# Twelve slots for expert weights and a reordered mixer tail in a two-layer hybrid trunk

## The chip, the cores and the metric

The kernel runs on one core of a Trainium2 chip. The metric is the device time of one execution in microseconds (us): 994.39 is the median of three runs of the kernel before (994.18 to 998.19). All arithmetic is float32.

## The reference

Two groups of 128 tokens, a prompt (g = 0) and latent tokens (g = 1), go through DEPTH = 2 layers of width 1024. Both groups use the same weights, so the kernel carries them side by side. One layer is:

```python
mod = silu(cond) @ w_ada[l] + b_ada[l]           # 6 parts of 1024: sh1, sc1, g1, sh2, sc2, g2
hn  = rmsnorm(x, norm_mix[l]) * (1 + sc1) + sh1
proj = hn @ w_in[l]                              # 3840 columns, split for three mixers
# differential attention (8 heads), retention (4), HGRN2 (4); each ends in an rmsnorm,
# retention and HGRN2 also times silu of a gate (r_g, g_g)
mix = concat(o_da, o_ret, o_hg) @ w_out[l]
x   = x + g1 * mix
hn  = rmsnorm(x, norm_ffn[l]) * (1 + sc2) + sh2
# router shared by all layers: 16 experts in 4 groups; the group with the largest sum of its two
# best scores, then its two best experts
x   = x + g2 * sum_e gate[e] * (silu(hn @ w_gate[l, e]) * (hn @ w_up[l, e])) @ w_down[l, e]
```

## The kernel before

**Weights.** All large weights go through `ring`, RING = 8 slots of 128 partitions x 2048 floats (1.049 MB each). SyncE issues every load (`load`, L353) in one fixed order, into slot `n % 8`, after the slot's last use has been counted; TensorE takes slots in the same order (`slot`, L430). The order in a layer is: w_in's blocks f, q, a, b, i, r, v, s with w_ada steps between them (ADA_BEHIND), the rest of the w_ada steps (LATER), w_out in eight half-filled slots, w_ada steps for the next layer (IN_ROUTER), and 96 expert slots. At the change of layers AT_CHANGE = 6 further w_ada steps come first (`at_change`, L551). A w_ada step (`ada_step`, L508) is one load and four products with a moving side of 512 columns.

**Engines.** Each engine runs its own list in the order in which it is written; semaphores tie the lists together, and after nearly each step an engine waits for its own result. PSUM has eight banks; projections and transposes of the mixers take banks 2, 3 and 0 in turn (`next_bank`, L574), scores take 4 to 7. There is no planner: the orders are written out by hand, TensorE's from L788 on, VectorE's from L1344, ScalarE's from L1706.

**Around the mixers.** The norm is folded into products: ScalarE squares and sums a group's rows (`squares`, L1585), VectorE scales a unit matrix by the result (`normed`, L1055), and TensorE multiplies x by this diagonal, which also transposes it (`normalized`, L478). VectorE and ScalarE shift and scale the result by feature into `hnT` (`shifted`, L1072 and L1607). Both groups are done one after the other before block f begins.

**The mixers' tail** (TensorE L864 to L885, VectorE L1391 to L1425, ScalarE L1742 to L1755). When the last values are there, `gated_norm` and `da_norm` fill `xs` with the mixed rows; `transposed("mix", ...)` (L873) turns them, in banks 0 and 3; VectorE copies group 0 and ScalarE group 1 to `hnT`; `copied("mix")` waits for all; then four sweeps of 256 columns for each group multiply by w_out, and VectorE adds `g1 * mix` to x, one quarter at a time. In layer 1 the second modulation (`modulation_by_feature`, L875) stands between the two groups' transposes.

**The turns.** The router gives each token two experts and a seat among 64 in each. The loop from L935 on does eight turns of two experts. A turn gathers the tokens of both experts (`gather`, a product with a 0/1 matrix), multiplies by w_gate and w_up (the two experts on the two halves of TensorE's columns), transposes the activations, multiplies by w_down, gathers for the next turn, and scatters the turn before it (`scatter`) into banks 4 to 7 in between. Each turn uses 12 slots: four of w_gate, four of w_up, four of w_down. The activation (VectorE L1515 to L1521) lies between w_up and w_down.

**After the turns** VectorE computes `x += g2 * y` in four pieces of 512 columns, two steps each (L1532 to L1540). Then the next layer's norm begins, or ScalarE issues the two output stores (L1783).

## Time and profile before

| what | before |
|---|---|
| median of 3 runs | 994.39 us |
| profiled execution, whole | 995.69 us |
| its span, first to last instruction | 993.9 us |
| granted TensorE clock, mean | 0.979 |
| PE busy | 932.2 us (94%) |
| PEld (weight loads into the array) busy | 507.4 us (51%) |
| DVE busy | 433.8 us (44%) |
| ACT busy | 158.8 us (16%) |
| POOL busy | 58.8 us (6%) |
| DMA | 303.63 MB, mean 305 GB/s |

The busy shares are averages over stages that are bound by different things. In the page's 40 slices of about 25 us, DMA moves 421 GB/s in the two long stretches in which the turns run and far less in the mixers of layer 1, while VectorE's share is high in the mixers and low in the turns. A busy matmul row can hide a short wait, since ends of matmuls are modelled; the chain of waits names such time "issue". In all rows times are in us from the start of the span, unless marked ns. PE is TensorE's matmuls, DVE VectorE, ACT ScalarE, POOL GpSimd, SPq SyncE's queue. A row's line (L421) can be that of a helper: L421 is every product, L454 every transpose, L361 every load of the ring. A float32 product is two instructions.

### The profile page before, as it was taken

How to read it: one execution, taken by the hardware profiler on the slowest of the kernel's cores; microseconds unless marked ns; L12 is line 12 of the kernel's file. 1: busy time of each engine (PE TensorE's matmuls, PEld its weight loads, DVE VectorE, ACT ScalarE, POOL GpSimd, SP SyncE). 2: the span in 40 equal slices, each digit the busy share in tenths (PEclk: the TensorE clock that was granted, in tenths of full speed). 3: DMA queues.
4: the chain of work that ended last, by engine and by line, in shares of the span. 5: the costliest groups of instructions: out<-in, count | busy, mean ns of one | idle time of the engine just before them, and what ended most of it. 6: DMA issues, size and time to landing. Idle time of an engine off the chain costs nothing.

```text
span 993.9 us, 13356 instructions
## 1 busy us (share of the span) xinstructions
PE 932.2 (94%) x5182; PEld 507.4 (51%) x5189; DVE 433.8 (44%) x792; ACT 158.8 (16%) x408; POOL 58.8 (6%) x92
## 2 busy tenths in 40 slices
PE   6899999999899999999989998998979999999996
PEld 2655574577543444443447567557863444443442
DVE  1386878533322222122347987863252222122222
ACT  2211043211100001010020203331120001010000
POOL 1112220020000000000000322000000000000000
PEclk9899999999999999999999999997989999999999
DMA  9997566478799999999996323312627999999992
GB/s 371 368 401 265 212 223 246 154 261 315 316 377 421 421 421 421 421 421 421 421 420 253 107 92 122 112 50 83 254 85 298 421 421 421 421 421 421 421 420 98
DMA packets 49582, 303.63 MB, mean 305 GB/s; under 512 B 7808, under 2 KB 7824, under 8 KB 17136
## 3 DMA queue, kind: packets, MB, share of 16 engines
q1 hardware_dynamic: 43520, 291.52, 72.7%
q0 software_dynamic: 2960, 8.63, 2.5%
q10 hardware_dynamic: 3040, 2.62, 0.8%
q8 instruction: 42, 0.69, 0.3%
q14 instruction: 20, 0.16, 0.0%
HBM read 300.10 MB, written 2.65 MB: 305 GB/s over the span
## 4 chain that ended last, share of the span: by engine, by line
PE 74%; DVE 16%; DMA 3%; ACT 3%; issue 3%; another core or an unknown queue 0%; SPq 0%; DVEq 0%; ACTq 0%
PE ps L421 72%; DMA ring<-in_w_ada 3%; PE ps L454 2%; ACT eP L1557 2%; DVE A L1235 1%; DVE rt L1033 1%; DVE xy L1229 1%; DVE eP L1333 1%; DVE stat L1033 1%; DVE eP L1331 1%; DVE F L1154 1%; DVE sq L1188 1%; DVE hnT L1081 0%; DVE proj L1262 0%; DVE xy L1160 0%
## 5 line engine op out<-in xcount | busy, mean ns | idle before, releaser
L421 PE MATMUL ps<-ring,proj 128*64 128x512 f32 x1536 | 339.4, 595 | 9.8 <-issue 8.0
L421 PEld LDWEIGHTS ps<-ring,proj 128*64 128x64 f32 x1536 | 109.8, 137 | 215.9 <-issue 213.9
L421 PE MATMUL ps<-ring,hnT 128*128 128x512 f32 (+1 forms) x576 | 204.5, 508 | 2.1 <-ACT hnT L1755 1.9
L421 PEld LDWEIGHTS ps<-ring,hnT 128*128 128x128 f32 x576 | 108.3, 193 | 75.8 <-issue 65.7
L421 PE MATMUL ps<-hnT,ring 128*64 128x128 f32 (+2 forms) x576 | 73.3, 338 | 0.0
L421 PEld LDWEIGHTS ps<-proj,xs 128*128 128x128 f32 x512 | 62.6, 203 | 16.0 <-issue 16.0
L421 PE MATMUL ps<-proj,xs 128*128 128x128 f32 x512 | 65.6, 290 | 4.2 <-issue 2.4
L421 PEld LDWEIGHTS ps<-hnT,ring 128*64 128x64 f32 (+1 forms) x576 | 59.9, 158 | 11.8 <-issue 2.4
L421 PE MATMUL ps<-proj 128*128 128x512 f32 x128 | 61.5, 606 | 0.0
L421 PE MATMUL ps<-ring,silT 128*32 128x512 f32 x384 | 48.3, 618 | 12.3 <-DVE silT L1049 7.5
L1527 DVE COPY proj<-ps 128x512 f32<-128x512 f32 x16 | 11.1, 692 | 109.1 <-PE ps L421 109.1
L1516 DVE TENSOR_SCALAR proj<-proj 128x512 f32<-128x512 f32 x16 | 6.8, 427 | 112.5 <-ACT proj L1557 112.5
L1517 DVE RECIPROCAL proj<-proj 128x512 f32<-128x512 f32 x16 | 53.6, 3353 | 0.5
L1569 ACT COPY proj<-ps 128x512 f32<-128x512 f32 x24 | 14.1, 586 | 161.7 <-PE ps L421 161.7
L421 PEld LDWEIGHTS ps<-proj 128*128 128x128 f32 x128 | 21.9, 190 | 29.2 <-issue 29.2
L421 PEld LDWEIGHTS ps<-xy 64*128 64x128 f32 (+1 forms) x480 | 30.0, 188 | 12.7 <-issue 11.8
L421 PE MATMUL ps<-xy 64*128 64x64 f32 (+1 forms) x480 | 32.2, 275 | 0.7 <-issue 0.6
L1777 ACT COPY proj<-ps 128x512 f32<-128x512 f32 x16 | 9.4, 586 | 146.3 <-PE ps L454 146.3
L1774 ACT COPY proj<-ps 128x512 f32<-128x512 f32 x32 | 18.8, 586 | 73.0 <-PE ps L421 73.0
L1235 DVE COPY_PREDICATED A<-c_later,ps 128x256 f32<-128x256 int32 x56 | 29.2, 521 | 1.9
L1557 ACT ACTIVATE eP<-ps,rt 128x128 f32<-128x128 f32 (+1 forms) x64 | 26.2, 418 | 23.6 <-DVE rt L1317 22.9
L1524 DVE COPY proj<-ps 128x256 f32<-128x256 f32 x16 | 6.8, 424 | 51.2 <-PE ps L454 51.2
(222 smaller groups left out, 751.2 us busy)
## 6 DMA issues: line engine op xcount, KB each, us to landing
ring<-in_w_gate SPq DMA_DIRECT2D x64, 1024.0 KB, 13.6
ring<-in_w_up SPq DMA_DIRECT2D x64, 1024.0 KB, 12.2
ring<-in_w_down SPq DMA_DIRECT2D x64, 1024.0 KB, 11.4
ring<-in_w_ada SPq DMA_DIRECT2D x48, 1024.0 KB, 8.3
ring<-in_w_in SPq DMA_DIRECT2D x28, 1024.0 KB, 7.5
ring<-in_w_out SPq DMA_DIRECT2D x16, 512.0 KB, 4.4
ring<-in_w_in SPq DMA_DIRECT2D x4, 512.0 KB, 12.6
xy<-gates POOLq DMA_DIRECT2D x4, 512.0 KB, 5.1
```

What stands on the lines that cost most here:

```text
L421: ins = nc.tensor.matmul(*a, **k)
L454: last = nc.tensor.transpose(ps[:, b, i * P:(i + 1) * P], src, C["ident"][:])
L1033: return v.tensor_reduce(out=out, in_=in_, axis=AX, op=op)
L1154: st(v.reciprocal(R, R))
L1188: st(v.reciprocal(e, e))
L1229: st(tt(keep, keep, other.broadcast_to([P, HR, P // (2 * b), b]), ALU.mult), "hX", g, lv + 1)
L1235: v.copy_predicated(out=half_blocks(A[:, g], lv, 1 - r), mask=mask, data=ps[:, bank, 0:256].rearrange("p (h n b) -> p h n b", h=HR, b=b)). ...
L1517: st(v.reciprocal(ge, ge))
L1527: v.tensor_copy(ys[:, 1], ps[:, 3]).then_inc(c.freed(("yP", 1), "ys", 1), 1)
L1557: return act_(out, in_, AF.Exp, scale=scale, **k)
L1569: (nc.scalar.copy(out, src) if fn is None else fn(src)).then_inc(c.freed(read, *label), 1)
L1774: evac(("xT", half), None, "xTs", half, fn=lambda src: nc.scalar.copy(xT[:, KH * half:KH * (half + 1), :], src.rearrange("p (k s) -> p k s ...
```

## The change

- **Slots.** The turns use twelve slots in the fixed order 4 to 11, 0 to 3: the eight of the ring and four made of buffers that are free during the turns (half of `eP`, `wT`, `F` with `A`, and `xy`, which holds the first gate until the first residual). SyncE waits for the first residual of group 1 before it issues the turns' loads. w_out is laid out as two halves of 512 columns, in four full slots; a slot is swept for two quarters.
- **w_ada.** AT_CHANGE becomes 5, and three steps instead of two stand behind block r in layer 1. Behind block v the steps go ahead of the end state. In the router's stage the steps are split 3, 1, 2, 2 instead of 2, 1, 1, 3, 1.
- **Norms group by group.** `normalized` becomes `normalized_group`. At the change of layers group 1 is normed between the halves of block f's first part. Before the router, VectorE builds group 0's diagonal ahead of the last residual step and group 1's after the first shifted half.
- **Mixers and tail.** VectorE does `query_columns(0)` ahead of `rotated_maps(1)` and evacuates block s ahead of `da_norm(1, 0)`; ScalarE takes the exponential for r_g of group 1 straight from PSUM. Layer 1's second modulation moves to where layer 0 has it. Group 0's transposes go to banks 6 and 7, ahead of the w_ada steps and the end state; each group's columns are copied half by VectorE, half by ScalarE; the first sweep of group 0 goes ahead of the transposes of group 1.
- **Router.** The group score is the largest of the six sums of two scores (three steps) instead of seven steps of minima and maxima.
- **Turns.** Seven products of zeros stand between the last rows and the loop. The gather for turn 1 goes into turn 0, behind w_up; from turn 1 on it stays behind w_down.
- **Second residual.** VectorE does the four products and the two sums of the upper halves, GpSimd the two sums of the lower halves. Each output store waits for its own group.

```diff
+TURN_SLOTS = (4, 5, 6, 7, 8, 9, 10, 11, 0, 1, 2, 3)
-ADA_BEHIND = ((2, 3, 3, 3, 3, 2, 3, 2), (0, 0, 0, 0, 0, 2, 0, 0))
-AT_CHANGE = 6
+ADA_BEHIND = ((2, 3, 3, 3, 3, 2, 3, 2), (0, 0, 0, 0, 0, 3, 0, 0))
+AT_CHANGE = 5
...
+            if s < RING:
+                return ring[:, s].rearrange("p k n -> p (k n)")
+            return (eP[:, 1], wT[:].rearrange("p a n -> p (a n)"), fa[:], xy[:].rearrange("p a h t -> p (a h t)"))[s - RING]
...
-                for i in range(4):
+                for half in range(2):
                     for r in range(2):
-                        load(lambda s: flat_slot(s)[:, 0:KH * 256], ap["w_out"][l, i, r])
+                        load(flat_slot, ap["w_out"][l, half, r])
                 if l + 1 < L:
                     for step in IN_ROUTER:
                         load_ada(*step)
+                sp.wait_ge(c.of("x1", 1), c.at("x1", 1))
...
+            def normalized_group(stage, factors, g, ahead=None, first=None):
+
+                xv = x[:, g].rearrange("p (k q) -> p k q", k=KC)
+                for h in range(2):
+                    b = claim_for_norm() if h or first is None else first
+                    if not h:
+                        if ahead is not None:
+                            ahead(b)
+                        pe.wait_ge(c.of(factors, g), c.at(factors, g))
+                    for k in range(KH):
+                        last = mm(ps[:, b, k * P:(k + 1) * P], xv[:, KH * h + k, :], diag[:, g, :], start=True, stop=True)
...
-                    normalized("hn1", "xn1", (at_change, None))
+                    normalized_group("hn1", "xn1", 0, at_change)
...
                     for g in range(NG):
+                        if l and g:
+                            normalized_group("hn1", "xn1", 1)
                         for hl in range(2):
...
                 da_weights(1, 0)
+                ada_behind("v")
                 end_state(1, "h", T_GI)
-                ada_behind("v")
...
-                if not l:
-                    modulation_by_feature(l, 1, next(turn_of_banks))
+                modulation_by_feature(l, 1, next(turn_of_banks))
...
                 ret_values(1)
+                transposed("mix", "mixed", 0, (6, 7))
                 ada_steps(len(LATER[l]))
                 end_state(0, "r", T_RV)
-                transposed("mix", "mixed", (0,))
-                if l:
-                    modulation_by_feature(l, 1, 2)
-                transposed("mix", "mixed", (1,))
-                copied("mix")
...
                 for n in range(4):
+                    if not n % 2:
+                        ss = [slot(), slot()]
+                    if not n:
+                        copied_group("mix", 0)
+                    out_of(n, 0, ss)
+                    if not n:
+                        transposed("mix", "mixed", 1)
+                        copied_group("mix", 1)
+                    out_of(n, 1, ss)
...
+                stream_zeros(0, 5)
+                mm(ps[:, 0, :], zeros[:, 0:P], zeros[:, 0:BLK], start=True, stop=True).then_inc(c.fills(0, "idle"), 1)
+                mm(ps[:, 0, :], zeros[:, 0:P], zeros[:, 0:BLK], start=True, stop=True).then_inc(S("bank0_free"), 1)
                 pe.wait_ge(S("rounds"), l + 2)
...
                         if t:
                             scatter(t - 1, 0)
-                            led.turn = t
+                        else:
+                            gather(1)
+                        led.turn = t
...
-                        if t + 1 < TURNS:
+                        if t and t + 1 < TURNS:
                             gather(t + 1)
...
+                query_columns(0)
                 rotated_maps(1)
-                query_columns(0)
...
+                evac_block("s")
                 da_norm(1, 0)
-                evac_block("s")
...
                 da_norm(1, 1)
+                mixed_columns(0)
                 gated_norm("ro", rnorm, 1, 24, 512, T_RG, "mixed", 1)
+                mixed_columns(1)
                 for n in range(4):
                     for g in range(NG):
                         sl = slice(n * 256, (n + 1) * 256)
+                        if n == 3 and g:
+                            normed("xn2", 0)
...
-                normed("xn2")
-                shifted("hn2", 1)
+                shifted("hn2", 1, ((0, 0),))
+                normed("xn2", 1)
+                shifted("hn2", 1, ((0, 1), (1, 0)))
...
+                dve.wait_ge(c.of("gate2"), c.at("gate2"))
                 for g in range(NG):
-                    for h in range(2):
+                    for h, to in enumerate((first_product[g], nsq[:])):
                         dve.wait_ge(c.of("y", 2 * g + h), c.at("y", 2 * g + h))
+                        tt(to, ps[:, 4 + 2 * g + h], gbuf2[:, g, h * BLK:(h + 1) * BLK], ALU.mult).then_inc(c.freed(("y", 2 * g + h), "x2p", g, h), 1)
                         dve.wait_ge(S(c.last[0]), c.last_value())
+                    st(tt(x[:, g, BLK:D], x[:, g, BLK:D], nsq[:], ALU.add), "x2", g)
...
+                    gathered(0)
                     for t in range(TURNS):
                         led.turn = t
                         acte.wait_ge(c.of("gu", 0), c.at("gu", 0))
                         st(ex_(ge, ps[:, 2], -1.0), "gexp")
+                        if not t:
+                            gathered(1)
+                            led.turn = t
                         evac(("actT",), None, "actTs", fn=lambda src: nc.scalar.copy(actT, src.rearrange("p (k s) -> p k s", k=KE)))
                         evac(("yP", 0), ys[:, 0], "ys", 0)
+                        if t and t + 1 < TURNS:
+                            gathered(t + 1)
...
+                    for g in range(NG):
+                        pool.wait_ge(c.of("x2p", g, 0), c.at("x2p", g, 0))
+                        put(g_.tensor_tensor(x[:, g, 0:BLK], x[:, g, 0:BLK], first_product[g], ALU.add), "x2a", g)
```

## Rows read from the trace of the kernel before

**Rows 1.** Windows of turns: length, PE, PEld, DVE, ACT, POOL busy, PEclk, DMA, GB/s

```profile
278.00:513.00 235.00, 227.99 (x1115) 96.30 (x1112) 64.41 (x86) 25.15 (x44) 0.00 (x0) 1.00 1.01 421
...
754.00:972.00 218.00, 211.71 (x1034) 91.17 (x1031) 57.47 (x75) 21.79 (x37) 0.00 (x0) 1.00 1.01 421
```

**Rows 2.** Chain that ended last, in order of time: start, length, what.

```profile
287.38 26.65 PE ps L421 x132
...
494.87 3.59 PE ps L421 x15
...
498.85 14.29 DMA ring<-in_w_ada
...
764.07 26.65 PE ps L421 x132
...
793.10 21.24 PE ps L421 x112
...
843.92 0.62 issue
...
972.75 7.07 PE ps L421 x32
```

**Rows 3.** Timeline: w_ada steps at the change; SyncE's first loads in turn 0.

```profile
506.45 3.64 PE L421 MATMUL ps<-ring,silT 128*32 128x512 f32 x32
...
751.20 4.62 SPq L361 DMA_DIRECT2D ring<-in_w_down  x4
```

**Rows 4.** Timeline, layer 1's norm and router; in brackets the idle time before.

```profile
719.61 2.02 PE L421 MATMUL ps<-t,x 128*128 128x128 f32 x16 [1.49 <-DVE t L1058]
...
732.37 0.17 DVE L1440 TENSOR_TENSOR rt<-rt 128x8 f32<-128x8 f32 x1
```

**Rows 5.** Timeline, first gathers, one in the steady state, turn 0's transposes.

```profile
265.49 5.42 PE L421 MATMUL ps<-proj,xs 128*128 128x128 f32 x32 [2.39 <-issue]
...
741.10 6.49 PE L421 MATMUL ps<-proj,xs 128*128 128x128 f32 x32 [1.82 <-DVE proj L1490]
...
762.30 0.88 PE L454 MATMUL ps<-c_begin,proj 128*128 128x128 f32 x6 [0.82 <-DVE proj L1521]
...
829.63 3.84 PE L421 MATMUL ps<-proj,xs 128*128 128x128 f32 x32
```

**Rows 6.** Timeline of TensorE, gaps in the mixers of both layers.

```profile
171.04 1.10 PE L421 MATMUL ps<-proj,kd 128*128 128x64 f32 x8 [1.58 <-DVE proj L1196]
...
606.71 2.09 PE L421 MATMUL ps<-kT,qT 32*128 32x128 f32 x32 [2.65 <-DVE qT L1305]
...
661.12 0.92 PE L454 MATMUL ps<-c_begin,eP 128*128 128x128 f32 x4 [1.93 <-DVE proj L1196]
...
662.27 4.85 PE L421 MATMUL ps<-ring,hnT 128*128 128x512 f32 x8
```

**Rows 7.** Timeline of TensorE, tail of the mixers, layer 0, then layer 1.

```profile
211.54 27.86 PE L421 MATMUL ps<-ring,hnT 128*128 128x256 f32 x128 [0.99 <-ACT hnT L1755]
...
679.10 1.94 PE L454 MATMUL ps<-c_begin,xs 128*128 128x128 f32 x8 [2.34 <-DVE xs L1287]
...
685.62 1.94 PE L454 MATMUL ps<-c_begin,xs 128*128 128x128 f32 x8 [1.38 <-DVE hnT L1415]
...
688.48 29.65 PE L421 MATMUL ps<-ring,hnT 128*128 128x256 f32 x128 [0.91 <-ACT hnT L1755]
```

**Rows 8.** GpSimd's products by form, then timeline: a collision, and the end.

```profile
L1833 POOL TENSOR_TENSOR e<-F 128x512 f32<-128x512 f32 x2 | 2.1, 1038 | 357.8 <-DVE xy L1175 357.8
...
572.98 0.67 POOL L1844 TENSOR_TENSOR xy<-xy,e 128x256 f32<-128x256 f32 x1 [3.96 <-PE ps L421]
...
573.02 0.91 DVE L1229 TENSOR_TENSOR xy<-xy,e 128x256 f32<-128x256 f32 x1 [1.18 <-PE ps L421]
...
988.80 0.69 DVE L1540 TENSOR_TENSOR x<-x,t 128x512 f32<-128x512 f32 x1
...
989.90 0.45 ACTq L1785 DMA_DIRECT2D out_o_ys<-x  x1
```

More of the change, by code:

```diff
@@ L457, in bank_of_transposes, with transposed @@
                 last.then_inc(c.fills(b, *label), 1)
-            def transposed(stage, rows, groups):
-                for g in groups:
-                    pe.wait_ge(c.of(rows, g), c.at(rows, g))
-                    xv = xs[:, g].rearrange("p (k q) -> p k q", k=KC)
-                    for h in range(2):
-                        bank_of_transposes((stage + "T", g, h), [xv[:, 4 * h + k, :] for k in range(4)])
+            def transposed(stage, rows, g, banks=(None, None)):
+                pe.wait_ge(c.of(rows, g), c.at(rows, g))
+                xv = xs[:, g].rearrange("p (k q) -> p k q", k=KC)
+                for h in range(2):
+                    bank_of_transposes((stage + "T", g, h), [xv[:, 4 * h + k, :] for k in range(4)], banks[h])
             def stream_zeros(b, n):
@@ L497, in copied_group @@
                     pe.wait_ge(c.of(stage + "S", g, h), c.at(stage + "S", g, h))
-            def copied(stage):
-                for g in range(NG):
-                    copied_group(stage, g)
             for b in range(8):
@@ L966, in _ @@
                             for half in range(2):
-                                pair = [slot(), slot()]
+                                pair = [slot(TURN_SLOTS[4 * i + 2 * half + e]) for e in range(2)]
                                 pe.wait_ge(c.of("xTs", half), c.at("xTs", half))
@@ L970, in _ @@
                                     for e, s in enumerate(pair):
-                                        last = mm(ps[64 * e:64 * e + 64, 2 + i, :], xT[:, KH * half + k, 64 * e:64 * e + 64], ring[:, s, k, :], start=(half == 0 and k == 0), stop=(half == 1 and k == KH - 1), skip_group_check=True)
+                                        last = mm(ps[64 * e:64 * e + 64, 2 + i, :], xT[:, KH * half + k, 64 * e:64 * e + 64], by_k(s, BLK)[:, k, :], start=(half == 0 and k == 0), stop=(half == 1 and k == KH - 1), skip_group_check=True)
                                         if k == KH - 1 and not (half and e):
@@ L992, in _ @@
                         for half in range(2):
-                            pair = [slot(), slot()]
-                            rows_of = [ring[:, s].rearrange("p k n -> p (k n)").rearrange("p (k n) -> p k n", k=KE // 2) for s in pair]
+                            pair = [slot(TURN_SLOTS[8 + 2 * half + e]) for e in range(2)]
+                            rows_of = [flat_slot(s).rearrange("p (k n) -> p k n", k=KE // 2) for s in pair]
                             for h in range(2):
@@ L1770, in _, with gathered @@
                     step[0] = "act_turn"
-                    for t in range(TURNS):
+                    def gathered(t):
                         led.turn = t
@@ L1902, in laid_out @@
     out = {"w_in": np.concatenate([halves(w_in[:, :, col:col + n], KH).reshape(L, -1) for _, col, n in IN_BLOCKS], 1)}
-    w_out = np.asarray(inputs["w_out"]).reshape(L, D, 4, 256).transpose(0, 2, 1, 3)
-    out["w_out"] = halves(w_out, KH).reshape(L, 4, 2, P, KH * 256)
+    w_out = np.asarray(inputs["w_out"]).reshape(L, D, 2, BLK).transpose(0, 2, 1, 3)
+    out["w_out"] = halves(w_out, KH).reshape(L, 2, 2, P, KH * BLK)
     for n in ("w_gate", "w_up"):
```

202 lines of the change are left out of this document (101 added, 101 removed).

## The prediction

> **What bounds the kernel now.** I read a table by stage first, then the chain of waits, and last the timeline around each idle stretch of TensorE. TensorE is busy in nearly all of the span, so what a change can win is its idle time, its slow-clock time, and whatever it waits for while it still counts as busy. The two stretches of expert turns (about 278 to 513 us and 754 to 972 us) have the DMA engines at a share of 1.01 and 421 GB/s beside a TensorE that is 97% busy [rows 1]. Which of the two sets the pace there? The chain shows it. The down projections of turns 0 and 1 of layer 1 start at 764.07 and 793.10, 29.03 us apart: that is TensorE's own pace. Later, "issue" pieces such as 0.62 us at 843.92 appear in the middle of the up projection, where nothing but a slot that has not landed can hold it. Over all seven periods layer 0 takes 494.87 - 287.38 = 207.5 us and layer 1 takes 972.75 - 764.07 = 208.7 us, against 7 x 29.03 = 203.2 [rows 2]. A turn loads 12 slots of 1.049 MB; at 421 GB/s that is 2.49 us each, 29.9 us a turn. So loads bind the turns by some 0.8 us each, and after layer 0 they still bind: the chain goes 14.29 us through a w_ada load before layer 1's first norm [rows 2].
> Outside the turns DMA has time to spare. There the chain alternates between TensorE and VectorE, and TensorE shows gaps at a handful of places, told below, with its clock at half beside some of them.
>
> **The change part by part.** I place each term on the profiled execution (995.69 us with what lies around its span of 993.9; the median of the runs shown is 994.39, 1.3 lower).
>
> *Twelve slots.* Before, the ring is eight deep: in layer 1 the first four loads after the ring was filled are issued only at 751.20, after the first gate half of turn 0 [rows 3], so DMA stood still before that. After, SP waits for the first residual and then has twelve slots for a turn. Is that wait harmful? In layer 1 it holds back 96 loads to about 22 us before the first gather (719.1 against 741.10, where the x1 sum ends about 0.5 us before the row at 719.61 [rows 4, 5]). 96 x 2.49 = 239 us after x1 the last load has landed. TensorE needs it, at its own pace, about 19 (to the first gather) + 4 (gather) + 26 (turn 0) + 174 (six turns at 29.03) + 22 us = 245 us after x1. Loads are ahead by some 4 us at the narrowest place. In layer 0 two w_ada loads go ahead of them and five behind (103 x 2.49 = 256 us), against about 261 us at which TensorE needs the last w_ada. So the turns should go at 29.03: -4.3 us in layer 0 and -5.5 in layer 1. Bounds: 0 (loads still bind) and these. I take the full value, since the margin comes out positive in both layers.
>
> *The change of layers.* AT_CHANGE of 5 takes one w_ada load out of the bound stretch and puts it behind block r, where its eight matmuls (0.9 us) lie in time that TensorE waits anyway. With loads on time TensorE's own work decides: the w_ada steps can begin 506.45 - 494.87 = 11.6 us after the last down does and take 0.91 each, 16.2 for five, in place of 498.85 + 14.29 - 494.87 = 18.3 and one step of 1.1 after it: -3.2 [rows 2, 3]. Norming group 1 between the halves of block f leaves VectorE's shifts of group 0 bare ahead of the first half; I give 0.9 back for that. Together -2.3 (0 to -4).
>
> *Mixers.* Layer 0: the three w_ada steps moved ahead of the end state cover the 1.58 us wait at 171.04: -1.6 (bounds 0 and -1.6). Layer 1: query_columns(0) ahead of rotated_maps(1) takes away the 2.65 us gap at 606.71, but VectorE (the swish reciprocals and the maxima) is next on that chain and is not shortened; only about 0.5 survives. Evacuating block s before da_norm(1, 0) takes the 1.93 us gap at 661.12, which layer 1's modulation product now fills; what is won is the clock, since the eight instructions after it took 4.85 us, where layer 0's 27.86 / 128 for 256 columns would make it 3.5: I take -1.2 [rows 6, 7]. Together -3.3, bounds 0 and -7.
>
> *Tail of layer 1's mixers.* From the end of the end state (679.10 - 2.34 = 676.8) to the end of the output projection (688.48 + 29.65 = 718.1) it is 41.4 us: waits of 2.34, 1.38 and 0.91, a modulation product of 3.2 (681.04 to 684.24) at half clock, two transposes of 1.94 each, and 29.65 of sweeps [rows 7]. After: group 0's transposes go to banks 6 and 7 and needn't wait for the gated norm of group 1; the modulation product is gone from here; the first sweep covers the norm of group 1. What is left is two transposes at full clock (2 x 1.3), one wait for the copies (0.99, as at 211.54 in layer 0) and sweeps at layer 0's 27.86: 31.5. That is -9.9. Bounds: -4 (only the modulation product leaves) and -11. Layer 0 has no such gaps, its w_ada steps fill them: 0. w_out's four full slots move the same bytes and are long there when needed: 0.
>
> *Norms and router.* With the norm group by group, layer 1's first diagonal is ready when the last sweep ends (the wait of 1.49 us at 719.61 goes), and the second about 0.5 earlier: -1.9. The seven small VectorE steps of the group scores are 0.2 us apart each and three replace them: -0.75. In layer 0 w_ada steps lie in the gaps, so -0.5 for the norms, -0.7 for the scores, and +1.0 for the step that is moved behind the seat count and there delays the last rows: -0.2. Sum -2.8 [rows 4], bounds -1 and -4.
>
> *Entry to the turns.* The first gather takes 5.42 and 6.49 us, while one in the steady state takes 3.84 [rows 5]: half clock after an idle wait. Seven zero products now stand in the wait. They cost 7 x 0.214 = 1.5 us, of which a part lies beside the loop entry (a gap of 1.8 to 2.4 us before those two gathers); I charge 0.9. So -1.6 + 0.9 and -2.65 + 0.9: -2.5. Bounds: +3.0 (the zeros in full, clock no better) and -4.3.
>
> *Turn 0.* The gather of turn 1 moves into the wait for `act` (0.82 before 762.30, and 0.9 between that row's end and 764.07 [rows 2, 5]), and ScalarE's two more copies delay the transposed activations by about half a microsecond: -1.2 for each layer, -2.4. Bounds +1 and -3.4.
>
> *Second residual.* VectorE has six steps of 0.72 us instead of eight. GpSimd's sum of 128x512 is 1.04 us [rows 8] and each can run beside VectorE's next product: -1.45 if nothing collides. The collision is seen in the trace: a 128x512 step of VectorE takes 0.69, so half the size should take about 0.4, but the 128x256 product with both inputs in SBUF took 0.91 at 573.02 as GpSimd's 0.67 us product ran at 572.98. I charge 0.8 for two such. The second group's store is now issued 0.4 us behind the last sum (989.90 against 989.49) and ends the span 4.0 us later, with the prompt's store beside it; with that one sent ahead it goes at once and lands alone, for which I take 1.5, a guess. Together -2.2, bounds -0.5 and -3.
> The Trainium skill, SBUF — State Buffer, Who interferes with whom, says that a VectorE instruction with two SBUF inputs and a GpSimd one that reads SBUF exclude each other, and that the products out of PSUM don't take part. By that rule both of VectorE's sums wait for GpSimd's; without it the end would come 0.8 us sooner. The trace's 0.91 agrees.
>
> Sum: -9.8 - 2.3 - 3.3 - 9.9 - 2.8 - 2.5 - 2.4 - 2.2 = -35.2, so 960.5 for that execution and **959 us** as a median.
>
> **Rivals.**
> *Loads still bind the turns.* For: the margins above are only 4 to 5 us in 240, and SP now issues no turn load before x1. Against: DMA idle time before the turns shrinks on both sides. Then turns and change give nothing: 959 + 12.1 = 971.
> *The mixers' chain catches the gain.* VectorE or ScalarE become late in the tail (both now copy mixed columns between steps of the gated norms). The mixers give 0 and the tail half: 959 + 3.3 + 5 = 967.
> *Only the outer edges move.* The reordering has a new wait in the mixers that eats as much as the tail gives, the loads are no longer early, and only norms, entry and end are left: 984 to 994.
> *Slower: the clock.* TensorE without its pauses is granted half clock in part of the turns. A us spent at half clock does the work of half a us, as gathers of 6.49 and 3.84 show [rows 5]. To eat 35 us it takes 70 us of turns at the lower level; a quarter of both stretches (116 us) would cost 58 us: 1017. Against: in both stretches the clock reads 1.00 at 97% busy [rows 1]. The lower level is seen only behind gaps.
>
> **How the numbers follow.** Forecast (all terms near their value, 950 to 965) 0.62; loads still bind 0.13; the chain catches 0.15; edges only 0.06; slower 0.04. Range 950 to 974: it takes in the first three. A measurement here tells 0.5% (5 us) from no change: faster 0.93, same 0.03, slower 0.04.
>
> **What would show it.** In the trace of after: downs 29.0 us apart in all seven periods of both layers and no "issue" piece of 0.6 us in the up projection; no w_ada load of many us in the chain at the change; no idle before the scores of group 0 in layer 1; about 31 us from end state to end of w_out in layer 1; first gathers of 3.8 us; the last VectorE sums stretched beside GpSimd's. Periods of 29.8 would make the turns' term wrong, a gap of over 2 us ahead of the output projection the tail's, and gathers over 5 us the entry's.

## The result, and the profile after

The changed kernel takes **962.53 us** (median of 4 runs, 962.35 to 963.17) beside 995.11 for the kernel before: a ratio of 0.9669, 95% interval 0.9646 to 0.9691, and 32.6 us less. The forecast was 959, range 950 to 974. The profiled execution has a span of 960.0 us (993.9 before), at a mean granted clock of 0.990 (0.979).

The page's busy times and TensorE's row of 40 slices: TensorE does its work in 6.5 us less busy time, and is busy for 96% of the span instead of 94%.

```profile
PE 925.7 (96%) x5205; PEld 500.9 (52%) x5205; DVE 431.9 (45%) x780; ACT 158.6 (17%) x408; POOL 63.6 (7%) x96
...
PE   6999999999999999999999999999989999999996
```

The turns, as windows (columns as in [rows 1]). TensorE has 0.85 us of idle time in 222 where it had 7.01 in 235, and DMA still moves 421 GB/s in layer 0's window, 410 in layer 1's.

```profile
278.00:500.00 222.00, 221.15 (x1082) 95.24 (x1082) 59.05 (x79) 21.75 (x37) 1.28 (x1) 1.00 1.01 421
...
735.00:945.00 210.00, 209.24 (x1030) 91.09 (x1028) 53.45 (x73) 21.15 (x36) 0.00 (x0) 1.00 0.99 410
```

The chain that ended last (start, length, what), against [rows 2]. Down projections start 28.96 us apart, from turn 1 (313.19) to turn 7 (486.94); no "issue" piece is left in them, and no w_ada load at the change of layers. The first row is of the mixers of layer 0; it is used further below.

```profile
127.94 0.70 DVE qT L1326
...
313.19 26.59 PE ps L427 x132
...
486.94 10.88 PE ps L427 x41
497.92 0.70 DVE t L1554
...
766.91 26.58 PE ps L427 x132
...
940.66 10.88 PE ps L427 x41
951.63 0.70 DVE t L1554
```

The timeline of TensorE, places in order of time: transposes in layer 0's mixers, first gather of layer 0, w_ada steps and norm at the change, the gap in layer 1's mixers and the w_ada steps behind it, and layer 1's tail (against [rows 5, 3, 6, 7]).

```profile
141.97 0.66 PE L461 MATMUL ps<-c_begin,proj 128*128 128x128 f32 x4 [0.71 <-DVE xs L1308]
...
264.87 3.84 PE L427 MATMUL ps<-proj,xs 128*128 128x128 f32 x32
...
498.39 4.50 PE L427 MATMUL ps<-ring,silT 128*32 128x512 f32 x40
503.61 2.05 PE L427 MATMUL ps<-t,x 128*128 128x128 f32 x16 [0.72 <-DVE t L1074]
...
606.17 0.66 PE L461 MATMUL ps<-c_begin,proj 128*128 128x128 f32 x4 [2.26 <-DVE xs L1308]
...
611.90 2.78 PE L427 MATMUL ps<-ring,silT 128*32 128x512 f32 x24
...
665.46 1.04 PE L461 MATMUL ps<-c_begin,xs 128*128 128x128 f32 x8
666.34 1.00 PE L427 MATMUL ps<-proj,kd 128*128 128x64 f32 x8
667.43 3.69 PE L427 MATMUL ps<-ring,hnT 128*128 128x256 f32 x16
670.96 1.04 PE L461 MATMUL ps<-c_begin,xs 128*128 128x128 f32 x8
672.73 11.49 PE L427 MATMUL ps<-ring,hnT 128*128 128x256 f32 x52 [0.73 <-ACT hnT L1690]
```

In the tail nothing waits between the values and the end of the first sweep; a transpose group of eight takes 1.04 where it took 1.94 at the lower clock. The end of w_out (697.18) is 31.7 us behind 665.46. The same stretch was 42.4 before.

Where the 33.9 us of the span went, from the distance between milestones in both traces (ends of sweeps, first gathers, down projections, last product; the cost of the products of zeros as e3 below measures it):

| step | predicted | measured |
|---|---|---|
| slots, turns 1 to 7, both layers | -9.8 | -10.6 |
| change of layers | -2.3 | -1.8 |
| from the start to the end of w_out, layer 0 | -1.6 | -1.9 |
| mixers, layer 1 (to the last values) | -1.7 | -0.6 |
| tail, layer 1 | -9.9 | -10.7 |
| norms and router, layer 0 | -0.2 | +0.9 |
| norms and router, layer 1 | -2.6 | -2.0 |
| entry to the turns, layers 0 and 1 | -2.5 | -1.2, -2.1 |
| turn 0, both layers | -2.4 | -2.1 |
| second residual and stores at the end | -2.2 | -1.8 |
| sum | -35.2 | -33.9 |

One more table is needed, for the granted clock. From 60 us on, TensorE is at its lower level (1.2 GHz) only in a few stretches, called episodes here; over windows that hold the shortest kind whole the mean reads 0.81 over 9 us or 0.79 over 8 us, which is 1.7 us of full clock lost. Adding up (1 - clock) x length over all windows of 4 us from 60 us to 960 us before, and to TensorE's last product at 952 us after, gives 15.4 us before and 3.4 us after. After, these are two episodes. Before, they are five stretches: three of 1.7 us, one of 3.4 (736 to 748), and one of 6.8 in the tail (676 to 693). Windows of TensorE in the kernel before (length, PE, PEclk, DMA share, GB/s), the second in the tail:

```profile
264.00:272.00 8.00, 6.51 (x38) 0.79 0.89 372
676.00:692.00 16.00, 11.36 (x47) 0.58 0.34 107
```

And after: the two that are left, and the tail.

```profile
252.00:260.00 8.00, 7.63 (x51) 0.79 1.01 423
603.00:612.00 9.00, 6.74 (x31) 0.81 0.07 30
668.00:684.00 16.00, 15.27 (x75) 1.00 0.23 75
```

So up to 12 of the 34 us are clock given back (up to, since a part of an episode can fall on idle time), over half of it in the tail (0.42 x 16 = 6.7), where the idle gaps were.

### The profile page after: what moved, and what is told of

Read it like the earlier page. It is cut to its first block, busy times and chain, and to the rows that moved or that the text cites. A ratio compares the mean times of both kernels' runs of the same rounds, so it can differ in the third digit from the quotient of the medians.

```text
span 960.0 us, 13408 instructions
## 1 busy us (share of the span) xinstructions
PE 925.7 (96%) x5205; PEld 500.9 (52%) x5205; DVE 431.9 (45%) x780; ACT 158.6 (17%) x408; POOL 63.6 (7%) x96
## 3 DMA queue, kind: packets, MB, share of 16 engines
HBM read 300.10 MB, written 2.65 MB: 315 GB/s over the span
## 4 chain that ended last, share of the span: by engine, by line
PE 85%; DVE 10%; ACT 2%; DMA 2%; issue 1%; SPq 0%; DVEq 0%; ACTq 0%
PE ps L427 83%; PE ps L461 2%; DMA ring<-in_w_ada 2%; ACT eP L1573 1%; DVE rt L1050 1%; DVE fa L1256 1%; DVE sq L1207 1%; DVE hnT L1098 1%; DVE xy L1250 1%; DVE stat L1050 1%; DVE x L1556 0%; DVE proj L1217 0%; DVE t L1295 0%; DVE proj L1283 0%; DVE nsq L1554 0%
## 5 line engine op out<-in xcount | busy, mean ns | idle before, releaser
L427 PE MATMUL ps<-ring,proj 128*64 128x512 f32 x1024 | 226.3, 595 | 1.0 <-ACT proj L1818 1.0
L427 PEld LDWEIGHTS ps<-ring,proj 128*64 128x64 f32 x1024 | 72.6, 137 | 132.8 <-issue 131.1
L427 PEld LDWEIGHTS ps<-proj,xs 128*128 128x128 f32 x512 | 58.4, 192 | 12.5 <-issue 11.4
L427 PE MATMUL ps<-proj,xs 128*128 128x128 f32 x512 | 61.4, 278 | 0.1
L427 PE MATMUL ps<-wT,proj 128*64 128x512 f32 x128 | 57.5, 592 | 0.0
L427 PE MATMUL ps<-fa,proj 128*64 128x512 f32 x128 | 57.5, 592 | 0.0
L427 PE MATMUL ps<-xy,proj 128*64 128x512 f32 x128 | 57.5, 592 | 0.0
L427 PE MATMUL ps<-eP,proj 128*64 128x512 f32 x128 | 57.5, 592 | 0.0
L1585 ACT COPY proj<-ps 128x512 f32<-128x512 f32 x24 | 14.0, 585 | 158.0 <-PE ps L427 157.9
L427 PEld LDWEIGHTS ps<-fa,proj 128*64 128x64 f32 x128 | 17.5, 137 | 36.1 <-issue 36.1
```

The costliest lines, as they stand in the source:

```text
L427: ins = nc.tensor.matmul(*a, **k)
L1585: (nc.scalar.copy(out, src) if fn is None else fn(src)).then_inc(c.freed(read, *label), 1)
```

## Experiments

Times are medians; the changed kernel is at 962.5 in its own runs, and the kernel before was at 995.5 to 996.2 in all of those below, 995.1 beside the changed kernel. "Ratio" is against the kernel before. The diffs are excerpts: "..." stands for what is left out, and where an edit has parts on several engines mostly TensorE's is shown.

**e1_ring8: the slots undone.**

```diff
-                                    load(flat_slot, half_experts[w][...], next(turn_slots))
+                                    load(flat_slot, half_experts[w][...])
-                                pair = [slot(TURN_SLOTS[4 * i + 2 * half + e]) for e in range(2)]
+                                pair = [slot() for e in range(2)]
-                sp.wait_ge(c.of("x1", 1), c.at("x1", 1))
```

> The changed kernel, but the turns take their twelve loads through the ring of eight slots, one after the other, as the kernel before does, and SP no longer waits for x1. Twelve slots theory (turns -9.8 us and the change of layers' w_ada in time, as the prediction charged): the stalls before down come back, the period between two down products rises above 28.96 us, turns 0 to 7 lose about 10 us, and TensorE waits again for w_ada at the change of layers, about 1 us; some 973 us. Rival (the loads kept up anyway, the gain came from what stands around the turns): 962 to 964 us, period unchanged.

975.56 us (974.85 to 977.48; ratio 0.9804, 0.9782 to 0.9826), so +13.0. Its chain has the stall back in every turn:

```profile
314.61 21.24 PE ps L425 x112
335.84 0.64 issue
...
344.42 21.24 PE ps L425 x112
...
493.90 7.03 PE ps L425 x31
500.94 13.51 DMA ring<-in_w_in
```

The period is 29.8 us. The six periods from turn 1 to turn 7 lose 5.5 and 5.2 us, turn 0 loses 0.7 and 0.8, and the change takes 2.6 us more, as TensorE waits for loads again: 0.52 us for w_ada and 2.07 us, which was not expected, for w_in.

**e5_slots_alone: the slots done alone, on the kernel before.**

```diff
+TURN_SLOTS = (0, 1, 2, 3, 8, 9, 10, 11, 4, 5, 6, 7)
+                sp.wait_ge(c.of("x1", 1), c.at("x1", 1))
-                                    load(flat_slot, half_experts[w][...])
+                                    load(flat_slot, half_experts[w][...], next(turn_slots))
```

> The kernel before with one part of the change alone: twelve slots in the turns (the oldest four of the ring first, then the four buffers of the mixers, then the other four) and SP's wait for x1. Prediction's terms for it: turns -4.3 and -5.5, and the w_ada waits at the change of layers, 1 to 2 us: -11 us against the kernel before, some 983 to 985 us; period between down products 28.96 us. Rival (the slots gain only with the rest of the change): -5 us or less.

984.41 us (983.37 to 986.89; ratio 0.9896, 0.9877 to 0.9916), -11.3. Period 28.96 us; all seven periods give 4.7 and 5.9 us and the change 1.4. Done alone or undone alone, the slots are worth 11 to 13 us: this part needs no other to work.

**e2_tail: the tail's order undone on three engines.**

```diff
-                transposed("mix", "mixed", 0, (6, 7))
                 ada_steps(len(LATER[l]))
                 end_state(0, "r", T_RV)
+                transposed("mix", "mixed", 0)
+                if l:
+                    modulation_by_feature(l, 1, 2)
+                transposed("mix", "mixed", 1)
...
```

> The changed kernel with the mixers' tail back in the order of before on TensorE, VectorE and ScalarE: both groups' transposes behind the end state, all columns copied before the first w_out sweep, layer 1's second modulation in the tail; w_out still in four full slots, norms still group by group. Tail theory: layer 1 from the end of ret_values to the last out sweep takes 41 to 42 us as before (31.7 in the changed kernel), layer 0 is as before within 1 us: +9 to +11 us, some 972 to 973 us. Rival (w_out in four full slots and the loads' time did it): +2 us or less.

The edit also puts `da_norm(1, 0)` ahead of the evacuation of block s again, and takes the second modulation out of layer 1's mixers, so TensorE's gap of 1.93 us is back there (at 651.09). 972.59 us (972.05 to 973.48; ratio 0.9775, 0.9755 to 0.9794), +10.1. TensorE's timeline and clock in the tail of this kernel; the waits and the half clock of before are back:

```profile
667.29 1.53 PE L461 MATMUL ps<-c_begin,xs 128*128 128x128 f32 x8 [2.26 <-DVE xs L1310]
668.61 3.41 PE L427 MATMUL ps<-c_begin,modX 128*128 128x4 f32 x16
673.31 1.97 PE L461 MATMUL ps<-c_begin,xs 128*128 128x128 f32 x8 [1.29 <-DVE hnT L1433]
676.06 8.29 PE L427 MATMUL ps<-ring,hnT 128*128 128x256 f32 x25 [0.78 <-issue]
```

```profile
252.00:260.00 8.00, 7.37 (x66) 1.00 1.01 425
668.00:684.00 16.00, 13.93 (x53) 0.58 0.28 74
```

The tail of layer 1 is 10.9 us longer than in the changed kernel, and the rows add up to that: idle gaps 3.6 (2.26, 1.29 and 0.78, less the 0.73 that the changed kernel keeps), the product's 1.8 at full clock, and 5.4 for the lower clock (1.4 on the transposes, 1.6 on the product, 2.4 on the sweeps, 30.54 against 28.14). Layer 0's tail, from the last values to the end of w_out, takes 35.2 us against 34.2, so the new order is worth 1.0 us there too, which the prediction had at 0. The first clock row shows something else: the clock stays whole at 252 to 260 us, where the changed kernel loses 1.7, and the first gather is 1.1 us *earlier* (263.80 against 264.87).

**e11_modulation_late: one part of the tail undone.**

```diff
-                modulation_by_feature(l, 1, next(turn_of_banks))
+                if not l:
+                    modulation_by_feature(l, 1, next(turn_of_banks))
...
                 end_state(0, "r", T_RV)
+                if l:
+                    modulation_by_feature(l, 1, 2)
...
```

> The changed kernel with one part of the tail undone: in layer 1 the modulation for the second norm is made in the tail again, behind the end state, on all three engines; everything else of the tail stays in its new order. The prediction charges the modulation product 3.2 us of the tail's 9.9; the order of the transposes and copies the rest. Theory: +3 to +4 us here (965.5 to 966.5), so that some 6 us are the order's. Rival (the modulation's chain over ScalarE, TensorE and VectorE is what all of the tail waited for): +8 to +10 us. Rival (the product goes under the wait for the copies): +1 us or less.

969.76 us (966.81 to 971.14; ratio 0.9735, 0.9714 to 0.9757), +7.2. That is between the 3 to 4 expected and the rival's 8 to 10, and fits neither. TensorE's timeline:

```profile
670.74 1.92 PE L427 MATMUL ps<-c_begin,modX 128*128 128x4 f32 x16 [2.11 <-ACT stout L1734]
672.52 5.39 PE L427 MATMUL ps<-ring,hnT 128*128 128x256 f32 x16
```

The tail is 5.5 us longer: 1.8 for the product, 2.1 of idle time ahead of it, as ScalarE first finishes the gated norm, and 1.7 on the sweep behind (5.39 against 3.69), which runs at the lower clock. The span is 8.4 us longer; the other 2.9 lie outside the tail, with clock episodes beside them that the changed kernel's profile has not (188 to 192 and 724 to 728). One small product thus brings its length, its wait, and the clock behind that wait; the order of transposes and copies is the other half. In layer 1's mixers the product costs next to nothing: from 616.9 to the last values the changed kernel takes 48.57 us, and this one, without it, 48.59.

**e3_nozeros: without the seven products of zeros.**

```diff
-                pe.wait_ge(S("bank0_free"), c.claim(0))
-                stream_zeros(0, 5)
-                mm(ps[:, 0, :], zeros[:, 0:P], ...).then_inc(c.fills(0, "idle"), 1)
-                mm(ps[:, 0, :], zeros[:, 0:P], ...).then_inc(S("bank0_free"), 1)
```

> The changed kernel without the seven products of zeros ahead of the turns of each layer. Clock theory: the first gather of a layer is again granted a low clock and takes 5.4 (layer 0) and 6.5 us (layer 1) instead of 3.84; it starts 0.3 and 0.66 us sooner; in sum +3.3 us by these, +2.4 by the prediction's own 0.9 a layer; 965 to 966 us. Rival (the earlier work already lifts the clock, the zeros only cost): -1 to -2 us.

965.75 us (963.28 to 966.62; ratio 0.9703, 0.9685 to 0.9721), +3.2; the profiled span is 961.5, +1.5. Its first gathers, then its clock at these and two other places:

```profile
264.30 5.46 PE L427 MATMUL ps<-proj,xs 128*128 128x128 f32 x32 [2.24 <-issue]
...
718.12 5.46 PE L427 MATMUL ps<-proj,xs 128*128 128x128 f32 x32 [1.91 <-DVE proj L1504]
```

```profile
264.00:272.00 8.00, 7.70 (x44) 0.79 1.02 422
603.00:612.00 9.00, 6.65 (x40) 1.00 0.17 66
718.00:726.00 8.00, 7.88 (x44) 0.79 1.01 422
```

Both gathers take 1.62 us more (6.5 us in all was expected in layer 1, it is 5.46) and start, counted from the end of w_out, 0.43 and 0.53 us sooner: the zeros are worth 1.1 to 1.2 us a layer. Layer 0's loss is there at turn 1 (314.25 against 313.19). It is gone again at the end of layer 1's mixers, since here the gap at 606 leaves the clock at 1.00.

**e4_gather_late: turn 1's gather back behind turn 0's down projection.**

```diff
-                        else:
-                            gather(1)
...
-                        if t and t + 1 < TURNS:
+                        if t + 1 < TURNS:
                             gather(t + 1)
...
```

> The changed kernel with turn 1's gather back behind turn 0's down products on TensorE and ScalarE. By the prediction, turn 0 loses 1.2 us in each layer, since nothing lies under the activations' way to the transposes; by the turns' measured ends 1.0 and 1.1: +2.1 to +2.4 us, 964.6 to 965 us. Rival (turn 0's gain came from the loads being there, not from the gather): within 0.5 us of 962.5.

965.49 us (962.64 to 968.02; ratio 0.9704, 0.968 to 0.9728); profiled span 960.9. From first gather to turn 1's down projection it takes 49.34 us in layer 0 (264.95 to 314.29) against 48.32, and 49.26 against 48.23 in layer 1: 1.0 us lost in each, as charged; the profiled execution gives 1.3 of it back at 606, where it too has the clock at 1.00. The median shows +3.0, within runs 5.4 us apart.

**e6_norm_both: group 1 normed ahead of block f again.**

```diff
                     normalized_group("hn1", "xn1", 0, at_change)
+                    normalized_group("hn1", "xn1", 1)
...
-                        if l and g:
-                            normalized_group("hn1", "xn1", 1)
...
```

> The changed kernel, but both groups are normed ahead of block f of layer 1 on TensorE and VectorE, as before. The prediction took 3.2 us for the change of layers and gave back 0.9 for norming group 1 between the halves of block f; measured were 1.6. If that 0.9 is a loss of the split, this kernel's first half of block f ends 0.9 us later but the second half starts at once, and the whole is 0 to 1 us faster; rival (the split lets TensorE start block f while group 1's sum is still on its way): 1 to 2 us slower, with TensorE waiting for x2 of group 1 at 505 to 507 us.

962.20 us (961.46 to 963.37; ratio 0.967, 0.9654 to 0.9686): no difference in the whole. (The 1.6 us that the expectation names are counted from the start of the w_ada steps.) From the last down projection to the end of the long row of block f it takes 71.1 us (485.22 to 556.35) against 69.75, 1.4 more. TensorE idles 1.31 us there ahead of the second norm, and the clock falls:

```profile
252.00:260.00 8.00, 7.42 (x62) 1.00 1.01 424
504.00:512.00 8.00, 6.51 (x64) 0.79 1.01 419
```

The split costs nothing: in this execution the old order is longer, by its wait and by the clock of 504 to 512. The 1.4 us are cancelled by the episode that this execution doesn't have at 252.

**e7_residual_dve: the second residual on VectorE alone.**

```diff
-                        tt(to, ps[:, 4 + 2 * g + h], ...).then_inc(..., "x2p", g, h), 1)
-                    st(tt(x[:, g, BLK:D], x[:, g, BLK:D], nsq[:], ALU.add), "x2", g)
+                        tt(to, ps[:, 4 + 2 * g + h], ...).then_inc(..., 1)
+                        st(tt(x[:, g, sl], x[:, g, sl], to, ALU.add), "x2" if h else "x2a", g)
...
-                        put(g_.tensor_tensor(x[:, g, 0:BLK], x[:, g, 0:BLK], first_product[g], ALU.add), "x2a", g)
```

> The changed kernel with the whole second residual on VectorE again, product and sum in turn as before; the stores stay one per group. Prediction: sharing it with GpSimd took 1.45 us off each residual and gave back 0.8 by the collision: +0.65 us at the change of layers and +0.65 at the end, VectorE's sums back at 0.69 us instead of 1.13 to 1.24; +1.3 us in all. Rival (the collision eats all of it): 0.

965.42 us (962.74 to 965.65; ratio 0.9693, 0.9674 to 0.9711), +2.9. At the two places themselves it is far less: from the last down projection to the first norm 17.11 us against 16.67, and from the first product to the last sum 5.77 against 5.27. Sharing is worth 0.44 and 0.50 us. The other 2.5 us of the span's 3.4 are there before the last down projection of layer 0, and far from the edit: 1.1 us before 50 us, and 1.2 in a clock episode at 188 to 194 us that the changed kernel's execution has not. The end of the changed kernel, in the timeline of all engines:

```profile
952.41 1.26 POOL L1875 TENSOR_TENSOR x<-x,t 128x512 f32<-128x512 f32 x1 [281.03 <-DVE t L1554]
953.09 1.13 DVE L1556 TENSOR_TENSOR x<-x,nsq 128x512 f32<-128x512 f32 x1
```

and of e10 below, in which the products go first:

```profile
957.47 1.26 POOL L1886 TENSOR_TENSOR x<-x,e 128x512 f32<-128x512 f32 x1 [0.25 <-DVE e L1561]
958.09 1.20 DVE L1556 TENSOR_TENSOR x<-x,nsq 128x512 f32<-128x512 f32 x1
959.32 0.69 DVE L1556 TENSOR_TENSOR x<-x,e 128x512 f32<-128x512 f32 x1
```

VectorE's sum takes 0.69 us alone. It overlaps GpSimd's by 0.58 us in the first fence and is 0.44 longer; by 0.64 in the second and is 0.51 longer. GpSimd takes 1.26 either way, also beside nothing but products out of PSUM, which stay at 0.69.

**e9_shift: the same work a microsecond later.**

```diff
+                    if not l and n == 1 and not g:
+                        stream_zeros(b, 5)
                     last = sweep(ps[:, b, 0:256], ...)
```

> The changed kernel with five products of zeros (1.07 us) ahead of one w_out sweep of layer 0, so that all behind it comes 1.1 us later and nothing else changes. The clock's drops at 254 to 260 us (0.50 to 0.83) and at 604 to 610 us (0.74) of the changed kernel are absent in kernels that reach these places about a microsecond apart from it. If the drops hang on when the place is reached, at least one is gone here, and the time is 0 to 2 us below 962.5 + 1.1; if they hang on the idle time ahead of them, both stay and the time is 963.6.

963.04 us (962.83 to 964.19; ratio 0.9679, 0.9663 to 0.9696). Its clock at both places:

```profile
252.00:260.00 8.00, 6.76 (x56) 1.00 1.01 427
603.00:612.00 9.00, 6.75 (x29) 0.81 0.15 61
```

This execution reaches the end of w_out 2.0 us later (0.93 of it from upstream of the edit) and the first gather only 0.66 later: 1.36 us come back, as the episode at 252 is absent. At 606 it remains.

**e10_three, e12_best, e13_fill: three tries at a better kernel.** e10 takes the gated norm ahead of the maxima in layer 1, e12 swaps two TensorE steps there instead, e13 fills the gap with zeros. All have the four last products ahead of the sums; e10 and e12 have a row transpose ahead of the router's second product (e12 in layer 0 only).

```diff
# e10
+                if not l:
+                    maxima(0, 0)
                 gated_norm("ho", hnorm, 0, 28, 768, T_GG)
+                if l:
+                    maxima(0, 0)
# e12
+                if not l:
+                    da_transposes(1)
                 by_head_pair(1, 1, ss, b)
+                if l:
+                    da_transposes(1)
# e13
+                if l:
+                    for _ in range(18):
+                        mm(ps[:, b, 256:512], zeros[:, 0:P], zeros[:, 0:256], ...)
                 da_transposes(1)
...
```

> The changed kernel with three edits: group 0's first row transposes go ahead of the router's transposed product (they fill TensorE's idle 0.6 us there); in layer 1 VectorE does the gated norm of group 0, which frees a bank that TensorE waits 2.26 us for at 606.17, ahead of the maxima of 2.30 us; in the last layer VectorE does all four products before its two sums, so that GpSimd's sums meet only products. Theory by these places: TensorE's gap at 606 falls to under 0.5 us and the clock stays at 1.00 there (-2.5 to -3 us); the router of layer 0 keeps its clock or waits for the picks instead (-1 to -2 us); the last sums take 0.7 to 1.0 us instead of 1.13 and 1.20 (-0.5 us): 957 to 959 us. Rival (the later maxima make the exponentials and layer 1's values late, or the gap moves to the next bank): gains at the router and the end only, 960.5 to 962 us.

> The changed kernel with three edits picked from the runs so far: in the last layer the four products go ahead of VectorE's two sums (that gave 0.45 us); in layer 0 alone group 0's first row transposes go ahead of the router's transposed product (0.66 us there); and in layer 1 the second half of block r's product for the second pair of heads goes ahead of the transposes of group 1, so that TensorE has 3.7 us of work where it waits 2.26 us for a bank at 606.17. Theory: no gap at 606 and the clock at 1.00 in 604 to 610, so layer 1's mixers 2.3 us shorter, and 1.2 more where the clock fell; 958 to 960 us. Rival (the transposes come 1.4 us later and group 1's scores and maxima with them, as the later maxima did in the run before): the gap moves behind 616 and the mixers gain nothing, 961 to 963 us.

> The changed kernel with two edits: in the last layer the four products ahead of VectorE's two sums (-0.45 us in the runs so far), and in layer 1 eighteen products of zeros (256 columns each, some 1.9 us in all) in TensorE's gap of 2.26 us ahead of the transposes of group 1, with no other order changed. If the idle gap is what lowers the clock in 603 to 612 us (0.81 to 0.84 over 9 us in four profiles, 1.00 in two with the same gap), it stays at 1.00 here and the time is 1.2 us lower still: 960.9 us, 960 to 961.5. Rival (the clock falls without regard to the gap): 962 us.

967.01 us (964.53 to 968.47; ratio 0.9713, 0.9695 to 0.973), 962.64 (962.14 to 965.99; 0.9669, 0.965 to 0.9688) and 963.50 (961.76 to 965.14; 0.9675, 0.9652 to 0.9697). None beats the changed kernel. The last sums end 0.45 us sooner in all three, and the gap at 606 is gone or mended in all. But each pays elsewhere. e12, timeline, then clock:

```profile
613.07 0.59 PE L427 MATMUL ps<-proj,fa 128*128 128x64 f32 x2 [1.95 <-ACT rkT L1749]
```

```profile
603.00:610.00 7.00, 7.00 (x46) 1.00 0.35 108
610.00:620.00 10.00, 8.05 (x36) 0.66 1.01 423
```

TensorE now arrives early at the next thing, ScalarE's copy behind its exponentials, waits 1.95 us there, and loses 3.4 us of clock (0.34 x 10). In e10 the exponentials start later as well, and it waits 3.42 us. e13's clock:

```profile
603.00:612.00 9.00, 8.65 (x59) 1.00 0.13 53
636.00:644.00 8.00, 7.81 (x32) 0.79 0.11 18
```

The clock holds at 606, as the theory wanted. One profile does not show that the zeros held it, since it holds in three of the nine profiles in which this gap is open (e1, e3 and e4). An episode comes at 636 here, behind an idle 1.23 us.

## Why the prediction was right, step by step

**Slots: right.** Periods are 28.96 us in both layers, and e1 and e5 bound the part from both sides. The margin that the prediction computed (4 to 5 us over a layer's loads) was enough, though no run measures its size: no load stops the turns. The rival "loads still bind" is excluded by the chain. Each layer gave 0.4 more than charged, as the six periods that the loads had held up go at 28.96 and not at 29.03.

**Change of layers: right in kind, 0.5 short.** The steps start 11.45 us after the last down projection and take 4.50, as predicted (11.6, and 0.91 each). The idle 0.72 us ahead of the norm, then 0.56, 0.31 and 0.67 in block f, are what was given back, about 1.5 where I charged 0.9. In e6's execution the old order idles as well, with half clock behind it. The w_ada step that went from the change to block r is not free, as the prediction had it: the three steps there follow one another without a gap (24 instructions in 2.78 us at 611.90; before, 16 in 1.92), and layer 1's mixers pay 0.9 us for it.

**Mixers: -2.5 for -3.3, and layer 0's part by luck.** The step that failed is "query_columns(0) ahead of rotated_maps(1) takes away the gap". In layer 1 the gap only moved, from the scores (2.65 us) to the transposes (2.26), with an episode of half clock behind it, as before. Block s did what was predicted: the eight instructions that took 4.85 us take 3.70, -1.2. Together with the 0.9 us of the moved w_ada step this gives the -0.6. Where the clock held at the gap (e3), the stretch from block f to the last values is 1.1 us shorter, and the term would be -1.7.

In layer 0 the same step costs time, which the prediction put at nothing. VectorE, which began the maps at once before, now waits 1.26 us for TensorE's transposes and copies the query columns first (127.94 in the chain); TensorE waits twice behind it (0.71 us at 141.97, and 0.48 at 148.42 where it was 0.20), and the stretch from 124.47 to 168.79 is 1.2 us longer than before. No run undoes this order alone. The order of block s costs 0.6 us more (e2 undoes it and has it back), the moved w_ada steps give 1.8, as charged with 1.6, and the tail gives 1.1. That adds up to -1.1. The rest of the -1.9, 0.8 us, is there already at 125 us, ahead of every reordered step of the mixers. It goes with an edit that neither the list of the change nor the prediction names: layer 0's five products of zeros ahead of block f stand ahead of the wait for its first load, no longer behind it. Before, TensorE idles 2.50 us at 30.75 and starts block f at 35.09; after, it starts it at 33.07. No run undoes this, and executions differ here anyway: the first w_ada step behind block f starts at 49.91 and 50.59 us in the two profiles with the old order (before and e5), and between 47.58 and 50.05 in the twelve with the new one.

**Tail: right, with the wrong split.** 10.7 for 9.9, and e2 gives 10.9 back. But the prediction counted it as gaps, a product of 3.2 us and slow sweeps one by one. The runs show 3.6 us of gaps, 1.8 of product and 5.4 of clock: with the gaps gone, the half clock is gone too, and it comes back when they do (e2). The modulation alone is worth 5.5 (product, wait and clock), not 3.2. "Layer 0: 0" was wrong by 1.0 us (e2).

**Norms and router: layer 1 right; layer 0 was the one sign that was wrong,** +0.9 for -0.2. The w_ada steps ahead of the seat count run at half clock in this execution (16 instructions take 3.58 us from 255.19, the next 16 take 1.92), so the picks wait for TensorE. e2, e6 and e9 have the clock at 1.00 there and take 1.36 us less from the end of w_out to the first gather, which would make the term -0.5. But the episode is not a rare accident: nine of the twelve profiles of the changed kernel and its variants have it in 252 to 264 us, so this order can be expected to pay for it.

**Entry: right, cheaper.** First gathers of 3.84 us as predicted; by e3 the zeros cost 0.43 and 0.53 us, not 0.9, and bring 1.62.

**Turn 0: right** (2.1 for 2.4), confirmed by e4 with 1.0 in each layer.

**Second residual: right but small.** Sharing gives 0.50 at the end by e7 where the prediction had 0.65; the rest of the 1.8 is the stores. The collision term was 0.8 and measures 0.95 (0.44 and 0.51). The Trainium skill (SBUF — State Buffer, Who interferes with whom) calls the shared ports an exclusive lock, by which a VectorE sum with two SBUF inputs would be held up by all of its overlap with GpSimd's. The trace has about 0.8 of that overlap (0.44 of 0.58, 0.51 of 0.64), and agrees that products out of PSUM are not touched.

The slower rival, the clock in the turns, can be excluded: the windows of turns stand at 1.00. "The mixers' chain catches the gain" is true of layer 1's mixers in part (-0.6 for -1.7), and not of the tail. The clock did matter, with the other sign, outside them.

The total is closer (-33.9 for -35.2) than the terms: in the mixers, the router and the tail, errors of 1 us of both signs cancel, and the clock decides several of them.

What stays open is what decides an episode. Nine profiles have the same gap ahead of the same transposes in layer 1 (606 us in the changed kernel), 2.25 to 2.35 us long. Behind it the clock falls in six (the changed kernel, e2, e6, e7, e9, e11) and holds in three (e1, e3, e4). So the gap alone doesn't decide it. When it is reached may matter; e9 was to show it and did for one place of the two, but a single execution with 0.93 us of shift from elsewhere is weak proof. The Trainium skill (TensorE: Matmul & The Clock Gate, Part 1) has the gate watch activity over a window that runs on by itself, which would make it a matter of phase; no run here controls that phase.

## What to carry to other kernels

Price an idle gap on TensorE at its length plus the clock that it can cost behind it: here 1.7 us an episode, often as much as the gap, and in six of nine profiles for the gap at 606 us. Take gaps away in runs, as the tail did, and not one at a time: a single gap that is closed shows up at the next late engine, as in e10, e12 and e13. And when parts are worth 1 us in a time whose executions differ by 3, read them off milestones in the trace at the place of the edit; medians of the whole would have credited e4, e7 and e11 with 1 to 2 us that are not theirs.

## What the runs showed of the hardware that I had not expected

- From 60 us on, each episode costs 1.7 us of full clock (0.79 over 8 us, 0.81 over 9) or close to a multiple of it where episodes follow one another directly (3.4 us in e12, 0.66 over 10; 6.8 in the tail before). The mean clock differs between executions of one kernel, and the span with it. e12's five have spans of 959.6, 959.7, 959.9, 963.3 and 963.8 us at mean clocks of 0.993, 0.991, 0.991, 0.987 and 0.985; e4's go from 960.8 at 0.995 to 966.1 at 0.987.
- e3 and e4 are 1.1 us late at the w_ada steps of the change of layers (499.44 and 499.48 against 498.39) and level with the changed kernel at the end of layer 1's mixers (665.44 and 665.30 against 665.46), because the episode at 606 is absent in both.
- GpSimd's 128x512 sum in SBUF takes 1.26 us, beside VectorE's sum or beside its products out of PSUM alone, against 1.04 for its product form [rows 8].
